# Feature blocks of three matmul operands placed 16, 64 and 8 bytes beyond multiples of 2 KB from each other

## The chip, the cores and the metric

The kernel runs on one core of a Trainium2 chip. The metric is the device time of one execution in microseconds (us), of which three runs are given. The profile is one further execution, seen by the hardware profiler.

## What is computed

Two transformer stacks run one behind the other on 512 tokens of width 1024, in float32. Each has two layers. The reference, cut to what the text speaks of:

```python
def first_block(x, ...):                     # 2 layers
    u = rmsnorm(h, attn_norm[l])
    h = h + hybrid_mixer(u, ...)             # three attention branches, gates, w_o
    u = rmsnorm(h, mlp_norm[l])
    h = h + jnp.square(jax.nn.relu(u @ w_up[l])) @ w_down[l]     # width 4096

def conv_ffn(h, w_up, w_dw, b_dw, w_down):   # second stack, width 2816
    u = depthwise_conv3(h @ w_up) + b_dw
    gate, val = jnp.split(u, 2, axis=-1)
    return (jax.nn.silu(gate) * val) @ w_down
```

The second stack also carries 256 context tokens (through its first layer, and as keys and values in its second).

## The kernel before

**Layout.** Activations lie in SBUF as features: a tile such as `xh` is `[128 partitions, 8 feature blocks (KT), 512 tokens (T)]`, so a feature block is 512 float32 values, 2048 bytes, of each partition, and the eight blocks follow each other without a gap. All weights come as slabs of 2048 values per partition (`wst`, two slots); a slab holds eight blocks of 256 output columns, so two output tiles of 128 columns.

**Arithmetic.** Every large product is made in three passes of the reduced float32 format F32R: an operand is split into a high part and the remainder (`whi`, `wlo` for weights; `xh`, `xl` for the normed input; `uh`, `ul` for the squared halves of the first stack's MLP; `gh`, `gl` for the gated halves of the second stack's; `mh`, `ml` and `oh`, `ol` elsewhere in the first stack; `xch`, `xcl`, `gch`, `gcl` for the 256 context tokens). ScalarE makes the high parts, VectorE (or GpSimd) the remainders. In `products` an output tile of 128 features by 512 tokens takes 24 matmuls: eight times `whi` by head and `whi` by tail (lines 812 and 813), then eight times `wlo` by head (line 816). The stationary operand is a 128x128 piece of a weight slab, the moving operand one feature block. Each matmul has a weight load of its own (LDWEIGHTS, shown as the engine PEld), which overlaps the matmul before it.

```python
for n, k in enumerate(first_ones):
    pe.matmul(out, weights(m.whi, k), head(k), start=opens and n == 0, stop=False)
    pe.matmul(out, weights(m.whi, k), tail(k), start=False, stop=False)
slab_rest()
for k in first_ones:
    last = pe.matmul(out, weights(m.wlo, k), head(k), start=False,
                     stop=closes and k == list(kts)[-1])
```

The same three terms stand in other helpers at lines 822 to 825, 983 to 988, 1060 to 1066 and, on 256 tokens of the second stack, 1290 to 1298. Lines 836 to 838 turn it round: there 128 tokens of `xh` or `xl` are the stationary operand, and `whi` or `wlo` moves.

**Order.** The program of each engine is written out by hand and joined by semaphores; nothing is scheduled by a planner. The DMA queue refills a weight slot when both parts of its slab are made.

**Addresses.** Tiles are placed by hand (`place`), each at the end of the last. `beside_weights(at)` rounds up to an address that is 128 modulo 512, which is also what the addresses of `whi` and `wlo` are; every 128x128 weight piece begins at such an address too, since pieces lie 512 bytes apart. `xh`, `xl`, `uh`, `ul`, `gh`, `gl`, `mh`, `ml`, `oh`, `ol` all begin there, and their blocks follow every 2048 bytes. `xch` and `gch` are placed 64 bytes beyond (`at + 64`), `xcl` and `gcl` right behind them, and their blocks follow every 1024 bytes. `ko` and `Qo` in the attention of the second stack, and `Kw` and `Qw`, are plain F32, and so are the transposes.

Of the kernel before, what the change touches and what calls it, by code (L numbers as in the profile page):

```python
# [23 lines left out]
P = 128  # L24
F32 = mybir.dt.float32
F32R = mybir.dt.float32r
# [6 lines left out]
KT = D // P  # L33
T = 512
# [156 lines left out]
TA = T + TC  # L191
# [222 lines left out]
def place(nc, at, name, shape, dt=F32):  # L414

    return nc.alloc_sbuf_tensor_at(name, shape, dt, offset=at), (at + 4 * int(np.prod(shape[1:])) + 31) // 32 * 32


def beside_weights(at):

    return at + (-at + 16512) % 512
# [7 lines left out]
def two_stacks(nc, io, out):  # L429
    m, s = Names(), Names()  # L430
    with ExitStack() as ctx:

        at = 16512
# [1 line left out]
        m.wst, at = place(nc, at, "wst", [P, 2, SLAB])  # L435
        m.whi, at = place(nc, at, "whi", [P, 2, SLAB], F32R)
        m.wlo, at = place(nc, at, "wlo", [P, 2, SLAB], F32R)
        m.xh, at = place(nc, at, "xh", [P, KT, T], F32R)
        m.xl, at = place(nc, at, "xl", [P, KT, T], F32R)
        m.cst, at = place(nc, at, "cst", [P, 258 + 2 * GATHER])  # L440
        m.sm1, at = place(nc, at, "sm1", [P, 75])
        m.nsink, m.rden, m.nmax = m.sm1[:, 42:58], m.sm1[:, 58:66], m.sm1[:, 66:70]
        m.mods, at = place(nc, at, "mods", [P, DEPTH, 6 * KT * 2])
        region = at = beside_weights(at)
        m.cosT, at = place(nc, region, "cosT", [P, T])
        m.sinT, at = place(nc, at, "sinT", [P, T])
        m.masks, at = place(nc, at, "masks", [P, MASKS])
        a_area = at = beside_weights(at)
        m.AQ, at = place(nc, at, "AQ", [P, 3, T])
        m.AK, at = place(nc, at, "AK", [P, T])  # L450
# [17 lines left out]
        m.mh, _ = place(nc, a_area, "mh", [P, KT, T], F32R)  # L468
        m.ml, _ = place(nc, a_area + 16384, "ml", [P, KT, T], F32R)
        b_area = at = beside_weights(at)  # L470
        assert a_area + 32768 <= b_area
        m.BQK, at = place(nc, at, "BQK", [P, 12, T])
        m.VB, at = place(nc, at, "VB", [P, QB, 12 * HD])
        m.oh, _ = place(nc, b_area, "oh", [P, 9, T], F32R)
        m.ol, _ = place(nc, b_area + 18432, "ol", [P, 9, T], F32R)
        m.uh, _ = place(nc, b_area, "uh", [P, KT, T], F32R)
        m.ul, _ = place(nc, b_area + 16384, "ul", [P, KT, T], F32R)
        work = at
        m.S4, at = place(nc, at, "S4", [P, 4, 4 * P])
        m.PT, at = place(nc, at, "PT", [P, 5, 4 * P])  # L480
        m.rows, at = place(nc, at, "rows", [P, 256])
# [41 lines left out]
        base2 = at = beside_weights(at)  # L523
# [18 lines left out]
        w2_area = at  # L542
# [4 lines left out]
        qs0, at = place(nc, at, "qs0", [P, T])  # L547
        ko1_area = at
        ko1, at = place(nc, at, "ko1", [P, TA])
# [4 lines left out]
        qol1, _ = place(nc, at - 4 * T, "qol1", [P, T], F32R)  # L554
# [17 lines left out]
        qs1, at = place(nc, at, "qs1", [P, T])  # L572
# [3 lines left out]
        ko0, _ = place(nc, ko0_area, "ko0", [P, TA])  # L576
# [2 lines left out]
        m.Kol, at = place(nc, region, "Kol", [P, 2, TA], F32R)  # L579
        qol0, _ = place(nc, at, "qol0", [P, T], F32R)  # L580
        m.Qol = qol0, qol1
        m.gh, at = place(nc, base2, "gh", [P, KT, T], F32R)
        m.gl, at = place(nc, at, "gl", [P, KT, T], F32R)
        m.gch, at = place(nc, at + 64, "gch", [P, KT, TC], F32R)
        m.gcl, at = place(nc, at, "gcl", [P, KT, TC], F32R)
        m.cg, at = place(nc, at, "cg", [P, T])
# [1 line left out]
        m.sgl, at = place(nc, at, "sgl", [P, T])  # L588
        m.gu, at = place(nc, at, "gu", [P, T])
        assert at <= 229344, at  # L590
        n_area = w2_area + 64
        m.sq2, _ = place(nc, n_area, "sq2", [P, 2, T])
        m.sum2, _ = place(nc, w2_area + 12288, "sum2", [P, TA])
        m.xn2, _ = place(nc, n_area + 4096, "xn2", [P, 2, T])
        m.rstd2, _ = place(nc, n_area + 8192, "rstd2", [P, TA])

        psum = ctx.enter_context(nc.psum_tensor("psum", [P, 8 * 512], F32))
        ps = [psum[:, 512 * b:512 * (b + 1)] for b in range(8)]
# [2700 lines left out]
```

## Time and profile before

| what | value |
|---|---|
| runs | 3473.51, 3473.83 and 3475.99 us, median 3473.83 |
| the profiled execution | span 3471.1 us from its first to its last instruction; no other time of it is given |
| TensorE matmul (PE) | busy 3371.9 us, 97% |
| weight loads (PEld) | 2790.2 us, 80% |
| VectorE (DVE) | 2072.0 us, 60% |
| ScalarE (ACT) | 1367.9 us, 39% |
| GpSimd (POOL) | 161.6 us, 5% |
| granted TensorE clock | 0.991 of full speed over the span |

A matmul's own duration in such rows (389 ns for 512 columns) holds its way through the array, which overlaps that of the next one. The time that a matmul costs is the distance from its start to the start of the next, called its pitch below. A row of the timeline that merges several matmuls gives the start of the first; the pitch is then the distance to the start of the row behind it, divided by their count. Engine names in rows: PE, PEld, DVE, ACT, POOL; L812 is line 812.

### The profile page before, as it was taken

How to read it: one execution, taken by the hardware profiler on the slowest of the kernel's cores; microseconds unless marked ns; L12 is line 12 of the kernel's file. 1: busy time of each engine (PE TensorE's matmuls, PEld its weight loads, DVE VectorE, ACT ScalarE, POOL GpSimd, SP SyncE). 2: the span in 40 equal slices, each digit the busy share in tenths (PEclk: the TensorE clock that was granted, in tenths of full speed). 3: DMA queues.
4: the chain of work that ended last, by engine and by line, in shares of the span. 5: the costliest groups of instructions: out<-in, count | busy, mean ns of one | idle time of the engine just before them, and what ended most of it. 6: DMA issues, size and time to landing. Idle time of an engine off the chain costs nothing.

```text
span 3471.1 us, 53538 instructions
## 1 busy us (share of the span) xinstructions
PE 3371.9 (97%) x20066; PEld 2790.2 (80%) x20066; DVE 2072.0 (60%) x3301; ACT 1367.9 (39%) x2166; POOL 161.6 (5%) x39
## 2 busy tenths in 40 slices
PE   8999999999999999999999999999999989999998
PEld 7766888888877678888888777988888878788887
DVE  7876457444678745655576655653544666556546
ACT  6556333222364553322222554342322346534323
POOL 2311000000133010000000000000000000000000
PEclk9999999999999999999999999999999999999999
DMA  4245232222222633332221001121121110122222
GB/s 144 85 158 205 101 121 102 96 96 96 90 103 88 240 124 122 108 119 96 93 92 49 25 14 57 49 73 61 61 73 49 73 61 26 57 69 101 97 97 85
DMA packets 45782, 317.13 MB, mean 91 GB/s; under 512 B 5008, under 2 KB 7312, under 8 KB 8464
## 3 DMA queue, kind: packets, MB, share of 16 engines
q1 hardware_dynamic: 44720, 307.07, 24.8%
q10 hardware_dynamic: 864, 7.31, 0.5%
q8 instruction: 138, 2.26, 0.3%
q14 instruction: 60, 0.49, 0.0%
HBM read 312.26 MB, written 2.10 MB: 91 GB/s over the span
## 4 chain that ended last, share of the span: by engine, by line
PE 84%; DVE 8%; ACT 3%; issue 2%; DVEq 1%; DMA 1%; POOL 0%; SPq 0%; ACTq 0%; POOLq 0%
PE psum L812 22%; PE psum L813 22%; PE psum L816 22%; PE psum L1470 3%; PE psum L1507 2%; PE psum L1491 2%; DVE MA L2478 1%; PE psum L1298 1%; PE psum L896 1%; ACT whi L1692 1%; PE psum L959 1%; PE psum L1290 1%; PE psum L1291 1%; PE psum L936 1%; PE psum L1433 1%
## 5 line engine op out<-in xcount | busy, mean ns | idle before, releaser
L812 PE MATMUL psum<-xh,whi 128*128 128x512 f32 (+1 forms) x2224 | 854.6, 386 | 2.7 <-issue 1.6
L813 PE MATMUL psum<-xl,whi 128*128 128x512 f32 (+1 forms) x2224 | 848.6, 384 | 0.0
L1692 ACT ACTIVATE whi<-wst 128x2048 fp32r<-128x2048 f32 x231 | 441.3, 1910 | 553.0 <-PE psum L816 531.9
L2224 DVE TENSOR_TENSOR wlo<-wst,whi 128x2048 fp32r<-128x2048 f32 x197 | 451.3, 2291 | 173.5 <-ACT whi L1692 171.8
L816 PE MATMUL psum<-xh,wlo 128*128 128x512 f32 (+1 forms) x2224 | 536.4, 383 | 0.1
L812 PEld LDWEIGHTS psum<-xh,whi 128*128 128x128 f32 x2224 | 418.6, 188 | 94.5 <-issue 13.5
L813 PEld LDWEIGHTS psum<-xl,whi 128*128 128x128 f32 x2224 | 418.5, 188 | 81.5 <-issue 1.0
L816 PEld LDWEIGHTS psum<-xh,wlo 128*128 128x128 f32 x2224 | 409.8, 188 | 82.3 <-POOL wlo L777 0.5
L777 POOL TENSOR_TENSOR wlo<-wst,whi 128x2048 fp32r<-128x2048 f32 x34 | 160.9, 4731 | 1081.4 <-ACT whi L1692 1081.1
L812 PE MATMUL psum<-uh,whi 128*128 128x512 f32 x480 | 186.9, 389 | 0.0
L813 PE MATMUL psum<-ul,whi 128*128 128x512 f32 x480 | 186.7, 389 | 0.0
L2083 ACT ACTIVATE S<-S,nmax 128x768 f32<-128x768 f32 (+1 forms) x120 | 101.8, 848 | 112.1 <-DVE rden L2983 85.0
L812 PE MATMUL psum<-gh,whi 128*128 128x512 f32 (+1 forms) x400 | 142.8, 366 | 1.0 <-DVE gl L3161 1.0
L813 PE MATMUL psum<-gl,whi 128*128 128x512 f32 (+1 forms) x400 | 142.2, 364 | 0.0
L1938 ACT ACTIVATE uh<-ur 128x512 f32 x64 | 40.5, 633 | 250.6 <-DVE ur L2726 250.6
L2746 DVE TENSOR_TENSOR hT<-hT,psum 128x512 f32<-128x512 f32 x64 | 43.8, 684 | 136.5 <-PE psum L816 119.5
L3082 DVE SCALAR_TENSOR_TENSOR hT<-psum,mod,hT 128x512 f32<-128x512 f32 (+1 forms) x80 | 51.1, 642 | 123.1 <-PE psum L816 123.0
L812 PE MATMUL psum<-xch,whi 128*128 128x256 f32 x488 | 121.0, 285 | 0.0
L813 PE MATMUL psum<-xcl,whi 128*128 128x256 f32 x488 | 120.3, 283 | 0.0
L816 PE MATMUL psum<-uh,wlo 128*128 128x512 f32 x480 | 119.2, 389 | 0.0
L2975 DVE CUSTOM_DVE_ANT_0 S<-psum,none 128x768 f32<-128x768 f32 (+1 forms) x120 | 101.4, 845 | 27.0 <-PE psum L1470 25.7
L1722 ACT ACTIVATE S<-S,sm 128x257 f32<-128x257 f32 (+5 forms) x144 | 80.4, 558 | 80.8 <-DVE sm L2427 79.2
(415 smaller groups left out, 5898.8 us busy)
## 6 DMA issues: line engine op xcount, KB each, us to landing
wst<-weights SPq DMA_DIRECT2D x287, 1024.0 KB, 4.8
dft<-c_dft ACTq DMA_DIRECT2D x2, 2688.0 KB, 10.1
hT<-x_t SPq DMA_DIRECT2D x4, 512.0 KB, 8.0
wst<-weights SPq DMA_DIRECT2D x2, 512.0 KB, 5.8
cT<-ctx_t ACTq DMA_DIRECT2D x1, 1024.0 KB, 7.0
out<-hT SPq DMA_DIRECT2D x1, 1024.0 KB, 4.9
out<-hT SPq DMA_DIRECT2D x2, 512.0 KB, 3.7
masks<-c_masks SPq DMA_DIRECT2D x1, 644.0 KB, 11.4
```

The lines of the kernel that those rows point to most:

```text
L777: nc.gpsimd.tensor_tensor(m.wlo[:, slab % 2, :], m.wst[:, slab % 2, :], m.whi[:, slab % 2, :].bitcast(F32), ALU.subtract).then_inc(s.lo_re ...
L812: pe.matmul(out, weights(m.whi, k), head(k), start=opens and n == 0, stop=False)
L813: pe.matmul(out, weights(m.whi, k), tail(k), start=False, stop=False)
L816: last = pe.matmul(out, weights(m.wlo, k), head(k), start=False, stop=closes and k == list(kts)[-1])
L1470: last = pe.matmul(ps[2 * par + c // 512][:, 0:w], q[a][:, q0:q0 + P], k[b][:, side * T + c:side * T + c + w], start=(a, b) == terms[0], s ...
L1491: last = pe.transpose(ps[bank][:, b * P:(b + 1) * P], m.S2[:, 2 * (u % 2) + b % 2, kb * P:(kb + 1) * P], ident)
L1507: mm = pe.matmul(ps[6][VH * par:VH * (par + 1), 0:P], m.V4[:, 4 * side + b // 2, col:col + VH], m.PT2[:, CHUNK2[l, u, c] % 5, (b % 4) * P: ...
L1692: act.activation(m.whi[:, slot, :], m.wst[:, slot, :], ACT.Copy).then_inc(s.hi_ready, 1)
L1722: act.activation(sc, sc, ACT.Exp, bias=m.nmax[:, 2 * (u % 2) + par:2 * (u % 2) + par + 1], scale=-1.0, accum_out=m.den[:, 2 * (u % 4) + pa ...
L2083: act.activation(sc, sc, ACT.Exp, bias=m.nmax2[:, 2 * (u % 2) + par:2 * (u % 2) + par + 1], scale=-1.0, accum_out=m.den2[:, c:c + 1]).then ...
L2224: TT(m.wlo[:, slot, :], m.wst[:, slot, :], m.whi[:, slot, :].bitcast(F32), ALU.subtract).then_inc(s.lo_ready, 1)
L2975: nc.vector.tensor_tensor_reduce(m.S2[:, at, 0:w], psum[:, 1024 * par:1024 * par + w], m.none[:, 0:1].broadcast_to([P, w]), -1.0, -TAKEN, ...
```

## The change

Six tiles get rows that are longer than what is used of them: `staggered` allocates `n + step` values for each block and hands out the first `n`. With steps of 4, 16 and 2 values, the blocks of `xh` and `xl` lie 2064 bytes apart, those of `uh` and `ul` 2112, those of `gh` and `gl` 2056. So block k begins 16k, 64k or 8k bytes beyond where it did, relative to its tile. `xl` begins 16512 bytes behind `xh` (128 beyond a multiple of 512 from it); `ul` and `gl` each begin 16896 bytes behind their partner, a multiple of 512. What lies behind the tiles moves: `cst`, `sm1` and `mods` by 256 bytes, `gch` to `gu`, `sq2` and `xn2` by 1024; everything from `region` on stays, for the rounding takes up the difference. `gch` stays 64 bytes beyond an address of the weights' kind. `rstd2`, which nothing reads, is gone. No instruction is added, removed or moved: each engine has as many rows in its program as before (9350 on PE, 2940 on DVE, 1695 on ACT, 10 on POOL, 21 on SP), and only line numbers and operand addresses differ.

```diff
+def staggered(nc, at, name, n, step):
+
+    tile, end = place(nc, at, name, [P, KT, n + step], F32R)
+    return tile[:, :, 0:n], end
...
-        m.xh, at = place(nc, at, "xh", [P, KT, T], F32R)
-        m.xl, at = place(nc, at, "xl", [P, KT, T], F32R)
+        m.xh, at = staggered(nc, at, "xh", T, 4)
+        m.xl, at = staggered(nc, at, "xl", T, 4)
...
-        m.uh, _ = place(nc, b_area, "uh", [P, KT, T], F32R)
-        m.ul, _ = place(nc, b_area + 16384, "ul", [P, KT, T], F32R)
+        m.uh, u_end = staggered(nc, b_area, "uh", T, 16)
+        m.ul, u_end = staggered(nc, u_end, "ul", T, 16)
         work = at
+        assert u_end <= work
...
-        m.gh, at = place(nc, base2, "gh", [P, KT, T], F32R)
-        m.gl, at = place(nc, at, "gl", [P, KT, T], F32R)
+        m.gh, at = staggered(nc, base2, "gh", T, 2)
+        m.gl, at = staggered(nc, beside_weights(at), "gl", T, 2)
+        at = beside_weights(at)
         m.gch, at = place(nc, at + 64, "gch", [P, KT, TC], F32R)
...
-        n_area = w2_area + 64
+        n_area = w2_area + 64 + 1024
         m.sq2, _ = place(nc, n_area, "sq2", [P, 2, T])
         m.sum2, _ = place(nc, w2_area + 12288, "sum2", [P, TA])
         m.xn2, _ = place(nc, n_area + 4096, "xn2", [P, 2, T])
-        m.rstd2, _ = place(nc, n_area + 8192, "rstd2", [P, TA])
```

## Rows read from the trace of the kernel before

**Rows 1.** The page: busy times, slices of the span, and the chain.

```profile
span 3471.1 us, 53538 instructions
PE 3371.9 (97%) x20066; PEld 2790.2 (80%) x20066; DVE 2072.0 (60%) x3301; ACT 1367.9 (39%) x2166; POOL 161.6 (5%) x39
PE   8999999999999999999999999999999989999998
PE 84%; DVE 8%; ACT 3%; issue 2%; DVEq 1%; DMA 1%; POOL 0%; SPq 0%; ACTq 0%; POOLq 0%
```

**Rows 2.** Stretches of 40 us: busy us and (count) by engine, clock, DMA.

```profile
1560.00:1600.00 40.00, 40.00 (x178) 33.14 (x177) 22.28 (x26) 11.77 (x12) 0.00 (x0) 1.00 0.28 100
3240.00:3280.00 40.00, 40.00 (x178) 33.14 (x177) 25.72 (x27) 17.05 (x20) 0.00 (x0) 1.00 0.28 94
```

**Rows 3.** Groups by line and shape: count, busy us, mean ns, idle before.

```profile
L812 PE MATMUL psum<-xh,whi 128*128 128x512 f32 x2096 | 822.9, 393 | 2.7 <-issue 1.6 <-DVE xc L2233 0.8 <-DVE ckvr L2789 0.2
...
L812 PE MATMUL psum<-uh,whi 128*128 128x512 f32 x480 | 186.9, 389 | 0.0
...
L812 PE MATMUL psum<-gh,whi 128*128 128x512 f32 x304 | 118.7, 391 | 1.0 <-DVE gl L3161 1.0
...
L1290 PE MATMUL psum<-xh,whi 128*128 128x256 f32 x256 | 64.8, 292 | 3.6 <-DVE xl L2337 3.6
...
L812 PE MATMUL psum<-xh,whi 128*128 128x256 f32 x128 | 31.7, 285 | 0.0
...
L812 PE MATMUL psum<-gh,whi 128*128 128x256 f32 x96 | 24.0, 286 | 0.0
...
L822 PE MATMUL psum<-uh,whi 128*128 128x512 f32 x32 | 12.4, 389 | 0.0
```

**Rows 4.** Timeline of PE in the first stack: start, us, instruction.

```profile
1499.62 0.39 PE L813 MATMUL psum<-xl,whi 128*128 128x512 f32 x1
1499.85 0.39 PE L812 MATMUL psum<-xh,whi 128*128 128x512 f32 x1
...
1502.57 1.98 PE L816 MATMUL psum<-xh,wlo 128*128 128x512 f32 x8
1504.38 0.39 PE L812 MATMUL psum<-xh,whi 128*128 128x512 f32 x1
```

**Rows 5.** Timeline of PE: 256 tokens of `xh`, blocks beside the weights.

```profile
2183.45 1.12 PE L816 MATMUL psum<-xh,wlo 128*128 128x256 f32 x8
2184.41 0.28 PE L812 MATMUL psum<-xh,whi 128*128 128x256 f32 x1
```

**Rows 6.** Timeline of PE: 256 tokens of `gch`, 64 bytes beyond.

```profile
2370.07 0.28 PE L812 MATMUL psum<-gch,whi 128*128 128x256 f32 x1
...
2371.72 0.98 PE L816 MATMUL psum<-gch,wlo 128*128 128x256 f32 x7
2372.54 0.40 PE L812 MATMUL psum<-gh,whi 128*128 128x512 f32 x1
```

**Rows 7.** Timeline of PE: `xch`, then the first matmuls of a `xh` tile.

```profile
2293.36 1.10 PE L816 MATMUL psum<-xch,wlo 128*128 128x256 f32 x8
2294.30 0.40 PE L812 MATMUL psum<-xh,whi 128*128 128x512 f32 x1
2294.54 0.39 PE L813 MATMUL psum<-xl,whi 128*128 128x512 f32 x1
2294.76 0.39 PE L812 MATMUL psum<-xh,whi 128*128 128x512 f32 x1
2294.99 0.40 PE L813 MATMUL psum<-xl,whi 128*128 128x512 f32 x1
2295.23 0.39 PE L812 MATMUL psum<-xh,whi 128*128 128x512 f32 x1
2295.46 0.40 PE L813 MATMUL psum<-xl,whi 128*128 128x512 f32 x1
2295.69 0.39 PE L812 MATMUL psum<-xh,whi 128*128 128x512 f32 x1
2295.92 0.39 PE L813 MATMUL psum<-xl,whi 128*128 128x512 f32 x1
2296.15 0.39 PE L812 MATMUL psum<-xh,whi 128*128 128x512 f32 x1
```

**Rows 8.** Timeline of PE: plain F32 logits (`ko`, `Qo`: 512, 256, 512, 256 columns).

```profile
1912.12 1.46 PE L1470 MATMUL psum<-ko,Qo 128*128 128x512 f32 x4
1913.41 0.60 PE L1491 MATMUL psum<-cst,S 128*128 128x128 f32 x4
```

**Rows 9.** Who waited for the matmuls of line 816 (us, times).

```profile
  ACT whi L1692: 531.9, 74
  ACT cv L2193: 150.8, 49
  DVE hT L3082: 123.0, 54
  DVE hT L2746: 119.5, 32
```

## The prediction

> **What bounds the kernel now.** I read the page first. TensorE is busy for 97% of the span, every slice but a few is full, and the chain that ended last is 84% PE [rows 1]. Next the stretches: within an MLP, PE is busy for all 40.00 of 40.00 us at a granted clock of 1.00 of full speed (the 2.4 GHz level), while DVE works 22 to 26 us and ACT 12 to 17, with the DMA engines at 0.28 [rows 2]. Then who waits for whom: ScalarE's next weight half and the residual additions of VectorE wait for PE's last matmul of a tile (531.9, 123.0 and 119.5 us in total) [rows 9], and not the other way round. So the end is set by how many matmuls there are and by the distance from the start of one to the start of the next. The change touches nothing but that distance.
>
> **The pitch before.** In the timeline of a long run of tiles the start moves from 1499.62 to 1504.38 us over 21 matmuls of 512 columns (13 single ones and the 8 merged), so 226.7 ns each [rows 4]. 512 columns at one column per cycle of 2.4 GHz are 213.3 ns. Each matmul therefore loses 13.3 ns, 5.9%, which no semaphore explains. Three things in the rows say what sort of loss that is:
>
> - It does not grow with the columns. `xh` with 256 columns: 2183.45 to 2184.41 us for 8 matmuls, 120.0 ns [rows 5], which is 13.3 ns above 106.7.
> - It changes with the address of the moving operand. `gch` has the same shape, the same weights and the same program around it, but lies 64 bytes beyond the weights' residue: 2370.07 to 2372.54 us for 21 matmuls, 117.6 ns [rows 6]. `xch`, with the same 64 bytes: 2293.36 to 2294.30 us for 8, 117.5 ns [rows 7]. That is 2.4 ns less per matmul. (Those blocks are also 1 KB long and not 2 KB apart; the rows don't separate the two.)
> - It hangs on the reading rate. Plain F32 takes two cycles a column: 1536 columns in four matmuls are 1.280 us, and they take 1912.12 to 1913.41, 1.29 us, so about 2.5 ns lost by each [rows 8].
>
> My reading: while a matmul streams a block at full rate, the weight load of the next one reads SBUF too, and some of its reads hold up the stream. How many do depends on how the two addresses run against each other. Before the change that relation is the same for every one of these matmuls, since pieces and blocks are all 128 modulo 512; after it every block k has its own.
>
> **A rule against this.** The Trainium skill says in "TensorE: Matmul & The Clock Gate", Part 2, that the moving operand and the weight load have independent read ports, so that loading weights takes nothing from the running matmul, and gives N/2.4 + 2.5 ns as the distance, 215.8 ns for 512 columns. By that rule addresses would not count and the time would stay at 3473.8 us. This trace disagrees with its figure for F32R (226.7 ns) and agrees with it for plain F32 (about 2.5 ns).
>
> **How much each ns is worth.** Matmuls of 512 columns that take one of the six tiles as moving operand: 2096 in each of the three terms for `xh` and `xl`, 480 in each for `uh` and `ul`, 304 in each for `gh` and `gl`, and 32 more in each for `uh` (the tile that is multiplied at line 822) [rows 3]. The rest of `xh` (lines 822 to 825, 983 to 988, 1060 to 1066) are 144, by the program. That is 6288 + 1440 + 912 + 96 + 144 = 8880 matmuls, 8.9 us for every ns of pitch; 6432 of them are `xh` and `xl`, 1536 `uh` and `ul`, 912 `gh` and `gl`. Of 256 columns there are (256 + 128 + 96) x 3 = 1440 [rows 3], 1.4 us per ns. Together they are 8880 x 226.7 + 1440 x 120.0 = 2186 us of the span.
>
> **The change part by part.**
>
> - The staggered starts of moving operands: the price has no row of its own. The nearest rows are the 64-byte tiles at 256 columns, 2.4 ns below the aligned ones [rows 5 to 7]. Since the loss does not grow with columns, I carry that over: 8880 x 2.4 = 21.3 us, and 1440 x 2.4 = 3.5 us. Sum: 24.8 us less.
> - Lower bound of the cost: the loss falls to the 2.5 ns of the plain F32 matmuls [rows 8]. 10.8 ns x (8880 + 1440) = 111 us less.
> - Upper bound: the row of unsettled pitches. After a switch from `xch` the first `xh` matmul takes 240 ns, and the six from 2294.54 to 2295.92 take 230 ns each, in an uneven order; only then it settles at 226.7 [rows 7]. If with eight different relations it never settles, 3.3 ns x 8880 = 29 us more.
> - `xh` and `xl` as stationary operand (lines 836 to 838, 192 matmuls), `cst` moved by 256 bytes, `gch` and the rest by 1024 with their residue kept: nothing. The first are too few (1 ns each is 0.2 us), the others keep the residue or are plain F32, which loses little anyway [rows 8].
> - VectorE's and ScalarE's writes of the six tiles at new starts: nothing. PE hides them; in the stretches DVE is idle for 14 to 18 of 40 us and ACT for 23 to 28 [rows 2]. They would have to grow by more than half before anybody waits.
> - A faster PE asks for slabs sooner. A slab lasts 48 matmuls, 10.9 us; its refill and its halves are covered by DMA at 0.28 and the idle shares above [rows 2]. So a gain on PE is passed on whole where PE is full, and I take it whole.
>
> The sum goes against the profiled span: 3471.1 - 24.8 = 3446.3 us. The median of the runs, 3473.83, is 2.7 us above that span; I add it: 3449 us, and round to 3450.
>
> **Rivals.**
>
> 1. *A small gain, as priced* (3450 us, faster). For: two tiles each side of a difference of 2.4 ns. Against: it is a constant offset there, and at 256 columns a weight load covers nearly the whole matmul, at 512 only the first half.
> 2. *A large gain* (3363 to 3435, say 3410). The aligned start may be the worst of all relations, each block and each part hitting it anew. If half of 13.3 ns goes, 6.7 x 8880 + 6.7 x 1440 = 69 us less, 3405. For: 2.5 ns shows that the loss can nearly vanish. Against: the 64 bytes took away only 2.4 of 13.3.
> 3. *Slower: the stream no longer settles.* Place: every 512-column tile of `xh`, two thirds of PE's matmuls of that kind. Price: pitch 230 instead of 226.7, 3474 + 29 = 3503 us; with 8 bytes (half of what a 16-byte step gives) for `gh` alone it would be only 3 us. For: right after a switch the pitch swings between 220 and 240 ns (the rows round to 10) and every mean over it lies above the settled one [rows 7]. Against: the 256-column tiles with another relation are faster, not slower. It decides when the mean pitch of staggered tiles is above 226.7.
> 4. *No change*: the loss belongs to the format, and the 2.4 ns at 256 columns come from the 1 KB blocks, not from the 64 bytes. Then nothing in the six tiles, whose blocks stay 2 KB long, gets cheaper: 3474 us. This is also where the skill's rule on separate ports would lead.
>
> **How the numbers follow.** A measurement of this kernel tells 0.2%, 7 us, from no change; that is 0.7 ns of pitch. Chances: case 1 0.40, case 2 0.22, case 3 0.23, case 4 0.15. Cases 1 and 2 are faster, 0.62; case 4 same, 0.14 with a little of it slower; slower 0.24. The range leaves out the lower part of case 2 (below 3390, more than 8 ns of pitch) and the upper part of case 3: from 3390 to 3490 us. Case 1 by itself would be 3435 to 3462.
>
> **What would show it.** In the profile after, the merged row of eight `xh` matmuls of line 816, from its start to the start of the next row and divided by eight: 224.3 ns if I am right, 226.7 if case 4 holds, 230 with visible swings for case 3, below 222 for case 2. `mh`, `ml`, `oh` and `ol` are not touched and must stay at 226.7. `gh` (8 bytes), `xh` (16) and `uh` (64) give three steps side by side: if the relation of addresses matters, they should differ. Busy PE should fall by what the span falls by, and DVE and ACT durations should stay. I am wrong if the pitch of all three tiles stays the same, or if the gain shows elsewhere than in these matmuls.

## The result, and the profile after

The changed kernel takes 3502.84 us (3500.40 to 3502.89, three runs) against 3473.83. The ratio is 1.0079, with a 95% interval of 1.0061 to 1.0097: 0.8% slower, 29 us, where 24 us less was forecast. That is the time of the rivals' case 3, which had been worked out at 3503 us; what is left of its reason is said below.

The page of the changed kernel, against [rows 1]. Its lines are numbered seven higher from the matmul helpers on (L812 is now L819, L813 L820, L816 L823).

```profile
span 3501.1 us, 53538 instructions
PE 3402.8 (97%) x20066; PEld 2784.8 (80%) x20066; DVE 2072.5 (59%) x3301; ACT 1367.0 (39%) x2166; POOL 160.6 (5%) x39
...
PE 85%; DVE 8%; ACT 3%; issue 2%; DVEq 1%; DMA 1%; SPq 0%; ACTq 0%
```

The span grew by 30.0 us and PE's busy time by 30.9; VectorE and ScalarE stay where they were. The loss lies in matmuls alone. The groups by line and shape (count, busy us, mean ns), against [rows 3]:

```profile
L819 PE MATMUL psum<-xh,whi 128*128 128x512 f32 x2096 | 831.7, 397 | 2.5 <-issue 1.6 <-DVE xc L2240 0.6 <-DVE ckvr L2796 0.2
L820 PE MATMUL psum<-xl,whi 128*128 128x512 f32 x2096 | 826.0, 394 | 0.0
L823 PE MATMUL psum<-xh,wlo 128*128 128x512 f32 x2096 | 525.9, 392 | 0.0
L819 PE MATMUL psum<-uh,whi 128*128 128x512 f32 x480 | 189.0, 394 | 0.0
...
L819 PE MATMUL psum<-gh,whi 128*128 128x512 f32 x304 | 119.9, 394 | 0.8 <-DVE gl L3168 0.8
L819 PE MATMUL psum<-xch,whi 128*128 128x256 f32 x488 | 118.1, 283 | 0.0
...
L819 PE MATMUL psum<-mh,whi 128*128 128x512 f32 x128 | 49.8, 389 | 0.0
```

Over its three terms `xh`/`xl` with 512 columns grew by 25.0 us, `uh`/`ul` by 5.8, `gh`/`gl` by 4.5. The untouched `mh` has its 389 ns and 49.8 us as before. Matmuls of 256 columns got cheaper, the 1440 on staggered tiles by 3.3 us together. `xch` and `xcl` won 6.6 us, although neither their addresses nor their program changed; `gch` and `gcl` lost 1.9.

These busy times hold each matmul's way through the array, so they don't add up to the span. Summed from start to start over all matmuls of the two traces, the account closes: `xh` and `xl` with 512 columns take 23.0 us more, `uh` and `ul` 6.3, `gh` and `gl` 4.5, all matmuls of 256 columns on the tiles named 4.5 less, everything else 0.5 more, together 29.8. By its settled pitch `xh` would have lost 30 us (4.7 ns on 6432 matmuls); 7 us of that don't show, 5 of them because fewer of its matmuls waited or ran at the 1.2 GHz level in this execution: 24 stood 400 to 440 ns from the next one before, 5 after.

The timeline of a long run, against [rows 4], shows the pitch: from 1509.93 to 1513.64 us 16 matmuls, then 8 in 1.84 us.

```profile
1509.93 0.39 PE L819 MATMUL psum<-xh,whi 128*128 128x512 f32 x1
1510.16 0.39 PE L820 MATMUL psum<-xl,whi 128*128 128x512 f32 x1
1510.39 0.40 PE L819 MATMUL psum<-xh,whi 128*128 128x512 f32 x1
...
1513.64 2.00 PE L823 MATMUL psum<-xh,wlo 128*128 128x512 f32 x8
1515.48 0.39 PE L819 MATMUL psum<-xh,whi 128*128 128x512 f32 x1
```

24 matmuls in 5.55 us are 231.3 ns each, where 226.7 stood. The median over all tiles of 24 is 231.4 ns for `xh`, 230.9 for `uh` and 232.5 for `gh`. Inside a tile the single distances swing between 225 and 237 ns; before they were 226 or 227.

### The profile page after: what moved, and what is told of

The parts are those of the page before. It is cut to its first block, busy times and chain, and to the rows that moved or that the text cites. A ratio compares the mean times of both kernels' runs of the same rounds, so it can differ in the third digit from the quotient of the medians.

```text
span 3501.1 us, 53538 instructions
## 1 busy us (share of the span) xinstructions
PE 3402.8 (97%) x20066; PEld 2784.8 (80%) x20066; DVE 2072.5 (59%) x3301; ACT 1367.0 (39%) x2166; POOL 160.6 (5%) x39
## 4 chain that ended last, share of the span: by engine, by line
PE 85%; DVE 8%; ACT 3%; issue 2%; DVEq 1%; DMA 1%; SPq 0%; ACTq 0%
PE psum L819 22%; PE psum L820 22%; PE psum L823 22%; PE psum L1477 2%; PE psum L1514 2%; PE psum L1498 2%; DVE MA L2485 1%; PE psum L903 1%; PE psum L1305 1%; PE psum L966 1%; ACT whi L1699 1%; PE psum L1297 1%; PE psum L1298 1%; DVE BQK L2249 1%; PE psum L943 1%
## 5 line engine op out<-in xcount | busy, mean ns | idle before, releaser
L819 PE MATMUL psum<-xh,whi 128*128 128x512 f32 (+1 forms) x2224 | 863.0, 390 | 2.5 <-issue 1.6
L820 PE MATMUL psum<-xl,whi 128*128 128x512 f32 (+1 forms) x2224 | 857.0, 388 | 0.0
L823 PE MATMUL psum<-xh,wlo 128*128 128x512 f32 (+1 forms) x2224 | 543.7, 386 | 0.0
L819 PEld LDWEIGHTS psum<-xh,whi 128*128 128x128 f32 x2224 | 417.5, 188 | 104.7 <-issue 13.3
L820 PEld LDWEIGHTS psum<-xl,whi 128*128 128x128 f32 x2224 | 418.4, 188 | 89.2 <-issue 1.0
L823 PEld LDWEIGHTS psum<-xh,wlo 128*128 128x128 f32 x2224 | 409.7, 188 | 89.3 <-POOL wlo L784 0.2
L819 PE MATMUL psum<-uh,whi 128*128 128x512 f32 x480 | 189.0, 394 | 0.0
L820 PE MATMUL psum<-ul,whi 128*128 128x512 f32 x480 | 188.4, 393 | 0.0
L819 PE MATMUL psum<-gh,whi 128*128 128x512 f32 (+1 forms) x400 | 143.7, 368 | 0.8 <-DVE gl L3168 0.8
L820 PE MATMUL psum<-gl,whi 128*128 128x512 f32 (+1 forms) x400 | 144.0, 369 | 0.0
L823 PE MATMUL psum<-uh,wlo 128*128 128x512 f32 x480 | 121.2, 393 | 0.0
L819 PE MATMUL psum<-xch,whi 128*128 128x256 f32 x488 | 118.1, 283 | 0.0
L820 PE MATMUL psum<-xcl,whi 128*128 128x256 f32 x488 | 117.3, 281 | 0.0
```

## The experiments

**How a pitch was measured by itself.** Five small programs hold nothing but TensorE's part: weights and blocks filled once, then tiles of 24 matmuls in the kernel's own pattern. They compute nothing of the reference. Each row of a table has its own source line, so each case is a group in the trace. In the first four programs it runs four tiles behind one tile of the plain layout; the fifth, in section 6, puts a tile of 512 columns before each tile of 256. The core of it:

```python
def case(n=512, at=0, step=0, gap=None, block=2048, w=0):
    pitch = block + step                      # bytes between blocks
    return n, at, pitch, KT * pitch if gap is None else gap, w
CASES = [
    ("plain", case(), lambda pe, *a, **o: pe.matmul(*a, **o)),
    ("osixteen", case(at=16), lambda pe, *a, **o: pe.matmul(*a, **o)),
...
    ("both", case(at=64, w=64), lambda pe, *a, **o: pe.matmul(*a, **o)),
```

**1. The first table.**

> A kernel of its own: TensorE alone, the kernel's 24-matmul pattern (hi by head and tail, then lo by head), four tiles per row of a table, each behind one tile of the plain layout. Each row of the table has its own source line. It computes nothing of the reference. Theory U (a relation of addresses that changes from matmul to matmul keeps the pitch from settling): with 512 columns the plain layout 226.7 ns; all blocks 8 to 1024 bytes off but 2048 apart also 226 to 227.5, since the relation is constant; steps of 8, 16, 32, 64, 128, 256 bytes 229 to 233; steps of 512 and 1024 bytes 226.7. Theory R (each relation of moving and weight address has its own price, and the aligned one is a cheap one): constant offsets of 16 to 256 bytes cost 229 to 233 as well, and moving the weights by the same 64 bytes as the blocks brings 226.7 back. Theory B (blocks that are not 2 KB apart cost, whatever the weights): steps of 512 and 1024 bytes cost 229 to 233 too. With 256 columns: 117.5 with 64 bytes of offset and 120.0 without, for blocks 2 KB and 1 KB apart alike, if the address makes that difference; else the 1 KB blocks alone show 117.5.

The timeline of this program; of each case the starts of its second and third tile, 24 matmuls apart. L25 is an offset of 16 bytes, L26 of 32, L29 of 256, L32 the tail alone 64 bytes on, L36 blocks with a step of 16, L41 with a step of 512, L43 weights alone 64 on, L44 weights and blocks both 64 on, L45 and L46 256 columns at offsets 0 and 64.

```profile
98.26 3.87 PE L25 MATMUL psum<-data,whi 128*128 128x512 f32 x16
...
103.82 3.87 PE L25 MATMUL psum<-data,whi 128*128 128x512 f32 x16
...
126.02 3.90 PE L26 MATMUL psum<-data,whi 128*128 128x512 f32 x16
...
131.62 3.90 PE L26 MATMUL psum<-data,whi 128*128 128x512 f32 x16
...
209.06 3.79 PE L29 MATMUL psum<-data,whi 128*128 128x512 f32 x16
...
214.50 3.79 PE L29 MATMUL psum<-data,whi 128*128 128x512 f32 x16
...
291.20 3.87 PE L32 MATMUL psum<-data,whi 128*128 128x512 f32 x16
...
296.76 3.87 PE L32 MATMUL psum<-data,whi 128*128 128x512 f32 x16
...
401.21 3.87 PE L36 MATMUL psum<-data,whi 128*128 128x512 f32 x16
...
406.76 3.87 PE L36 MATMUL psum<-data,whi 128*128 128x512 f32 x16
...
538.92 3.79 PE L41 MATMUL psum<-data,whi 128*128 128x512 f32 x16
...
544.37 3.79 PE L41 MATMUL psum<-data,whi 128*128 128x512 f32 x16
...
593.48 3.90 PE L43 MATMUL psum<-data,whi 128*128 128x512 f32 x16
...
599.08 3.90 PE L43 MATMUL psum<-data,whi 128*128 128x512 f32 x16
...
621.23 3.79 PE L44 MATMUL psum<-data,whi 128*128 128x512 f32 x16
...
626.67 3.79 PE L44 MATMUL psum<-data,whi 128*128 128x512 f32 x16
...
645.88 2.08 PE L45 MATMUL psum<-data,whi 128*128 128x256 f32 x16
...
648.76 2.08 PE L45 MATMUL psum<-data,whi 128*128 128x256 f32 x16
...
662.82 2.05 PE L46 MATMUL psum<-data,whi 128*128 128x256 f32 x16
...
665.64 2.05 PE L46 MATMUL psum<-data,whi 128*128 128x256 f32 x16
```

A constant offset is not free: 5.56 us over 24 is 231.7 ns at 16 bytes, 5.60 is 233.3 at 32. At 256 it is 226.7 again, and so are steps of 256, 512 and 1024 bytes. Weights moved alone give 233.3 (5.60 us), weights and blocks moved together 226.7. Theory U had constant offsets at 226 to 227.5 ns and theory B had costly steps of 512 and 1024 bytes; neither is so. R stands, but for its 229 to 233 ns at 256 bytes: the price repeats after 256 bytes.

A change of relation from one matmul to the next is not free either. With the tail alone 64 bytes on, 16 of 24 matmuls stand at offset 0 and 8 at 64, which by the prices of constant offsets would be 227.4 ns in the mean; 5.56 us over 24 are 231.7. With the tail 16 bytes on, 228.3 would be the mean and 231.1 was measured; at 128 bytes the mean of prices, 228.9, is met.

With 256 columns 64 bytes save 2.3 ns (120.0 to 117.6), for blocks 1 KB or 2 KB apart alike: the prediction's reading of rows 5 and 6 was right. At 512 columns the same 64 bytes cost 2.2 ns.

**2. Undoing the largest part; a constant offset in the kernel.** `x_plain` puts the two `staggered` calls of `xh` and `xl` back to `place`. `all_64`:

```diff
-        m.xh, at = place(nc, at, "xh", [P, KT, T], F32R)
+        m.xh, at = place(nc, at + 64, "xh", [P, KT, T], F32R)
...
-        m.gch, at = place(nc, at + 64, "gch", [P, KT, TC], F32R)
+        m.gch, at = place(nc, at, "gch", [P, KT, TC], F32R)
```

and the same 64 bytes for `uh`, `ul` and `gh`.

> The changed kernel with xh and xl put back to blocks 2048 bytes apart; uh, ul, gh and gl stay staggered. By the pitches of the changed kernel's trace xh and xl hold some 29 us of the loss on 6432 matmuls of 512 columns, against a few us that 256-column matmuls win, so 3476 to 3482 us. Rival (the loss comes from uh, ul, gh, gl or from the tiles that moved): 3495 us or more.

> The kernel before with xh, xl, uh, ul, gh and gl each begun 64 bytes further on and blocks still 2048 bytes apart, so that the moving operand is always 64 bytes off the weights' residue. Theory U: the relation is constant, so the 512-column pitch stays 226 to 227.5 ns and the time within 7 us of before, at most 3 us less by the 256-column matmuls. Theory R (any relation but the aligned one costs): pitch 229 to 233 and 3495 to 3520 us. The prediction's own price (64 bytes save 2.4 ns of every matmul): 224.3 ns and 3450 us.

`x_plain`: 3486.86 us, ratio to before 1.0037 (1.0023 to 1.0051). So the loss is there in part without the `xh` stagger, and `xh` holds 18 us of the span (3501.1 to 3482.9), not the 21 to 27 forecast: by busy time its 512-column matmuls gave back 25 us, but `xch` and `xcl` lost the 6.5 that they had won. `all_64`: 3487.77 us, 1.0035 (1.0024 to 1.0045), pitch 228.8 by its timeline (8 matmuls from 1664.09 to 1665.92 us, 1.83 us over 8), near the 228.9 that the first table has for 64 bytes. U had said at most 3482, R at least 3495, so neither range of times is met. R's took a dearer offset than the table gives; by the table it is 2.2 ns on 8880 matmuls less 2.3 on 1440, 16 us, and 13 were measured between the medians (3474.58 to 3487.77). The prediction's own 224.3 ns and 3450 us are refuted.

**3. The scan, and a stagger that keeps the residue.**

> TensorE alone as in the first table, none of the reference computed. With 512 columns: 24 to 248 bytes and 320 of constant offset between blocks and weights; with 256 columns ten offsets; with 128, 384 and 448 columns offsets 0, 64 and 192; weight pieces of 64 and 32 columns in place of 128; and 32 plain F32 matmuls each at offsets 0, 64 and 128. Theory R (the price hangs on moving address minus weight address modulo 256): 320 bytes cost what 64 cost, 228.9 ns, 192 bytes what the weights moved by 64 cost, 233.3; no offset is below 226.7 with 512 columns. Theory L (each line of the weight load that meets the stream costs about one cycle of 2.4 GHz, so the loss scales with weight columns): pieces of 64 columns 219 to 221 ns, of 32 columns 215 to 218. If the loss belongs to the format, it stays 13.3 ns there. Plain F32: 429 ns at every offset. With 384 and 448 columns the aligned loss is 13.3 ns too; with 128 the weight load is as long as the matmul and the pitch is its own.

```diff
-        m.uh, _ = place(nc, b_area, "uh", [P, KT, T], F32R)
-        m.ul, _ = place(nc, b_area + 16384, "ul", [P, KT, T], F32R)
+        uh, u_end = place(nc, b_area, "uh", [P, KT, T + 64], F32R)
+        ul, u_end = place(nc, u_end, "ul", [P, KT, T + 64], F32R)
+        m.uh, m.ul = uh[:, :, 0:T], ul[:, :, 0:T]
```

> The kernel before with uh and ul alone staggered, their blocks 2304 bytes apart (256 bytes beyond 2 KB in place of the change's 64), which keeps every block at the weights' address modulo 256. Theory R: pitch 226.7 on uh and ul and the time within 2 us of before (3472 to 3477). Theory U (any block by block change of relation unsettles the pitch): 230 to 231 ns on 1536 matmuls, 5 to 7 us more, 3479 to 3482 us.

`u_256`: 3473.99 us, 0.9998 (0.9989 to 1.0007), and `uh` at the pitch of before. Its group, against 121.2 us with 64 bytes of step and 119.2 before:

```profile
L817 PE MATMUL psum<-uh,wlo 128*128 128x512 f32 x480 | 119.2, 389 | 0.0
```

A block-by-block change of 256 bytes costs nothing. The prices of this scan and of the first and third tables, settled pitch in ns at 512 columns, by blocks' minus weights' address:

| bytes | 0 | 4 | 8 | 12 | 16 | 24 | 32 | 40 | 48 | 64 | 80 | 96 |
|---|---|---|---|---|---|---|---|---|---|---|---|---|
| ns | 226.7 | 236.7 | 233.3 | 229.2 | 231.7 | 233.0 | 233.3 | 232.5 | 233.3 | 228.9 | 231.1 | 233.3 |

| bytes | 112 | 128 | 144 | 160 | 176 | 192 | 208 | 224 | 240 | 256 | 320 | 1024 |
|---|---|---|---|---|---|---|---|---|---|---|---|---|
| ns | 231.1 | 233.3 | 233.3 | 234.3 | 231.1 | 233.3 | 234.7 | 233.3 | 233.3 | 226.7 | 228.9 | 226.7 |

Of 31 offsets tried below 256 bytes (those not shown lie between 230.8 and 234.8) none is cheaper than the aligned one. At 256 columns it is among the dearest: 120.0 at 0, 96 and 128, 118.7 at 16, 116.7 at 32, 118.3 at 48, 117.8 at 64 and 192, 117.1 at 240. At 448 columns 64 bytes give 200.0 against 202.7; at 384 both give 173.3, and 192 bytes 176.7. So the sign of an offset's price depends on the columns. The loss of the aligned layout against one column per cycle of 2.4 GHz is not 13.3 ns throughout either, as had been forecast: it is at 384 columns, but 16.0 at 448.

Theory L falls. Fewer weight columns make it slower: with weights of 64 columns (L58, first and fourth tile) 72 matmuls in 16.56 us are 230.0 ns; with 32 columns (L59) two tiles stand 5.55 us apart, 231.3, and the mean over its tiles is 231.7.

```profile
841.04 3.84 PE L58 MATMUL psum<-data,whi 128*64 128x512 f32 x16
...
857.60 3.84 PE L58 MATMUL psum<-data,whi 128*64 128x512 f32 x16
...
874.12 3.87 PE L59 MATMUL psum<-data,whi 128*32 128x512 f32 x16
...
879.67 3.87 PE L59 MATMUL psum<-data,whi 128*32 128x512 f32 x16
```

Plain F32 is the same at offsets 0, 64 and 128: 429.1 ns from record to record. (32 matmuls show as 64 records; each record is half of a plain F32 matmul. Rows 8 are four such halves, two of 512 columns and then two of 256, so the 2.5 ns lost by each record stand, but a matmul has two of them.)

**4. Is it the difference alone, and can context tiles gain?**

> TensorE alone as in the first tables, none of the reference computed. (1) Blocks and weights both 128 or both 192 bytes on, and weights 256 on with blocks 64: theory R (the price hangs on the difference alone) 226.7, 226.7 and 233.3 (difference -192 is 64: 228.9); blocks 128 with weights 64 as a difference of 64, 228.9; weights 192 on with plain blocks as -192, so 64, 228.9. (2) Further constant offsets between 4 and 232 bytes: none below 226.7. (3) One block used by all matmuls, or one for head and one for tail: 226.7 at offset 0 and the same prices at 16 to 128 as with eight blocks (231.7, 233.3, 228.9, 233.3), if the relation to the weights alone counts; other prices if it is the relation of one block to the next. (4) The same weight piece for all eight: 226.7. (5) Weight pieces read with a stride of two values, so that their address runs as fast as the moving one: no forecast from R; if the loss comes from the two addresses passing each other, the pitch falls at some offset below 226.7. (6) 256 columns with blocks 1 KB apart: 116.7 at 32 bytes, 117.7 at 64.

All of theory R's forecasts are met: 226.7 with both 128 or both 192 on; 228.9 with blocks 128 and weights 64 on, with weights 192 on, and with weights 256 and blocks 64 on; and two blocks, one for all heads and one for all tails, show 226.7, 231.7, 233.3, 228.9 and 233.3 at 0, 16, 32, 64 and 128 bytes. So where the offset is constant, the distance from one block to the next plays no part. Weights read with a stride of two: 231.5 to 233.3, no offset helps.

> The kernel before with xch, xcl, gch and gcl 32 bytes beyond the weights' residue in place of 64, blocks 1 KB apart as before. By the scan 32 bytes give 116.7 ns at 256 columns against 117.7 at 64, on 664 x 3 = 1992 matmuls: 2 us less, 3472 us, less than a run can tell. Rival (the pitch there is set by how a tile starts, not by the offset): no row of 116.7 and 3474 us.

`ctx_32` (each of the four context tiles 32 bytes earlier): 3474.19 us, 1.0000 (0.9991 to 1.0009). The row of 116.7 is there in most `xch` tiles (67.2 us for 488 `wlo` matmuls against 67.6), and as forecast a run cannot tell it.

**5. Which weight load, and does the table carry over?**

> TensorE alone as in the first tables, none of the reference computed. Which weight load meets a stream: that of the next matmul (theory N, the reading of the prediction) or the matmul's own (theory O)? In the rows own64, own128 and own16 every second matmul has block and weights both 64, 128 or 16 bytes on; in next64, next128 and next16 the block of a matmul matches the weights of the one behind it. N: next64, next128 and next16 226.7 ns, and own64, own128 and own16 above it. O: the reverse. weights and blocks rows move one side of every second matmul alone; both theories 228 to 231. steps: blocks and weight pieces both staggered by 16 bytes; O 226.7, N about 231, since the piece behind is always 16 bytes further. 96 columns of weights at offset 0 between 226.7 and 230.0, by the two rows measured for 128 and 64. 480 to 504 columns: 213 to 224 ns, a loss of 13 to 16 ns like that at 448 and 384.

Neither theory: with 64 bytes own and next both 231.7, with 128 bytes 228.3 and 230.0, with 16 bytes 233.3 and 230.5; moving only the weights of every second matmul by 16 bytes costs nothing (226.7), by 128 bytes it gives 233.3. Staggering blocks and weights alike gives 229.4. In the own rows and in this last one every block agrees with its own weights, and yet they cost 1.7 to 6.7 ns: the difference of a matmul's two addresses sets the price alone only where it and the addresses' residue stay the same from matmul to matmul. Of the other forecasts, weights of 96 columns came out at 230.0, the upper end; 480 and 496 columns at 216.7 and 220.0; 504 columns at 226.7, above the 224 allowed. The reading "the next weight load disturbs the stream" is neither shown nor refuted by these pairs; a simple rule of own or next load is. The rows own64 (L24) and next64 (L25), second and third tile:

```profile
71.75 3.87 PE L24 MATMUL psum<-data,whi 128*128 128x512 f32 x16
...
77.31 3.87 PE L24 MATMUL psum<-data,whi 128*128 128x512 f32 x16
...
99.44 3.87 PE L25 MATMUL psum<-data,whi 128*128 128x512 f32 x16
...
105.00 3.87 PE L25 MATMUL psum<-data,whi 128*128 128x512 f32 x16
```

> The kernel before with xh, xl, uh, ul, gh and gl each begun 32 bytes further on, blocks 2048 bytes apart. If the table of prices carries over to the kernel: 233.3 ns on 8880 matmuls of 512 columns, 59 us more; 116.7 instead of 120.0 ns on 1440 of 256 columns, 5 us less; so about 3528 us, 3518 to 3533. If constant relations are cheap in the kernel, under 3490.

`all_32` (as `all_64`, with 32; `gch` keeps its 64): 3518.26 us, 1.0123 (1.0105 to 1.0141), at the lower end of the forecast. Its settled pitch is the table's: the median over tiles of 24 is 233.3 ns for `xh`, `uh` and `gh` alike (228.9 in `all_64`). The groups of its `wlo` matmuls show the price on the moved tiles, and none on `mh`:

```profile
L816 PE MATMUL psum<-xh,wlo 128*128 128x512 f32 x2096 | 531.9, 395 | 0.0
L816 PE MATMUL psum<-uh,wlo 128*128 128x512 f32 x480 | 122.3, 395 | 0.0
...
L816 PE MATMUL psum<-mh,wlo 128*128 128x512 f32 x128 | 32.2, 389 | 0.0
```

**6. Untouched context tiles that got faster.** Eleven times in the kernel 96 matmuls of `xch` and `xcl` follow each other, ten times of them behind a tile of 512 columns. These ten go at 113.3 ns in the changed kernel, where all eleven go at 117.8 before; in `x_plain` they are back at 117.8.

> TensorE alone, none of the reference computed. Tiles of 256 columns, 64 bytes off the weights, each behind a tile of 512 columns, as the context tiles stand in the second stack. In the changed kernel untouched context tiles run at 113 ns where before they run at 118, so a constant relation seems to have more than one settled pitch, and the tile in front to choose. If so, a row whose tile in front lies 16, 32 or 128 bytes off, or is staggered by 16, shows 113 where the aligned one in front shows 118; and perhaps another offset of block 0, block 7 or the tail tips it over with an aligned tile in front, which a kernel could use: 4.4 ns on up to 1992 matmuls, 9 us. Rival: the 118 stands in every row with an aligned tile in front, and only the offsets within the tile change it, by what the scan gave (116.7 to 120).

In the small program the forecast holds in part: behind an aligned tile of 512 columns the 64-byte tile settles at 117.9 ns; behind one at 64 bytes, or staggered by 16, at 113.3; behind one at 16 or 128 bytes at 117.9. Behind one at 32 bytes (L23; the start of the 256-column tile and of the next 512-column tile) the first of four still ran at 117.9 and the other three at 113.3:

```profile
72.42 2.05 PE L23 MATMUL psum<-data,whi 128*128 128x256 f32 x16
...
75.25 3.88 PE L115 MATMUL psum<-data,whi 128*128 128x512 f32 x16
...
80.84 1.98 PE L23 MATMUL psum<-data,whi 128*128 128x256 f32 x16
...
83.56 3.89 PE L115 MATMUL psum<-data,whi 128*128 128x512 f32 x16
```

2.83 us and 2.72 us for the same 24 matmuls: one relation of addresses, two settled pitches. The kernels bear out a part of it: in `all_32` the same ten go at 113.3 as well, but in `all_64`, where `xh` is 64 bytes off, they stay at 117.8. Of one of them the starts of the first and second tile (24 matmuls in 2.82 us, 117.5 ns each):

```profile
2292.34 0.28 PE L812 MATMUL psum<-xch,whi 128*128 128x256 f32 x1
...
2295.16 0.28 PE L812 MATMUL psum<-xch,whi 128*128 128x256 f32 x1
```

So the offset of the tile in front is not all that chooses; what else does was not found. With an aligned tile in front, block 0 alone at the weights' residue gave 115.0 over the tile. That was tried in the kernel:

```diff
-        m.xch, at = place(nc, at + 64, "xch", [P, KT, TC], F32R)
+        xch, at = place(nc, at, "xch", [P, 16 + KT * TC], F32R)
+        m.xch = Blocks(xch, [0] + [16 + k * TC for k in range(1, KT)], TC)
```

> The kernel before with block 0 of xch alone put at the weights' own residue, the other seven and all of xcl left 64 bytes off; all else as before. In the table of entries this took a 256-column tile behind an aligned 512-column tile from 117.9 to 115.0 ns a matmul. xch has 488 x 3 = 1464 matmuls: 4.2 us less, 3470 us, about half of what a run can tell, so the pitch in the trace has to show it: 113 to 115 ns in the tiles of xch in place of 117.5. Rival: in the kernel the tile in front ends otherwise than in the small program, the pitch stays at 117.5 to 118 and the time at 3474.

`ctx_first`: 3475.63 us, 1.0002 (0.9993 to 1.0011), no difference that a run can tell. In the trace the starts of the first three of four tiles of `xch` that follow each other:

```profile
2289.42 0.28 PE L824 MATMUL psum<-xch,whi 128*128 128x256 f32 x1
...
2292.18 0.28 PE L824 MATMUL psum<-xch,whi 128*128 128x256 f32 x1
...
2295.00 0.28 PE L824 MATMUL psum<-xch,whi 128*128 128x256 f32 x1
```

The first tile takes 2.76 us, 115.0 ns each, as in the small program; the second 2.82 us, and by the starts 117.4 and the two behind it 117.5. So the effect of block 0 did carry over, but only to a tile right behind one of 512 columns: 13 tiles have it, 312 of 1464 matmuls, worth 0.9 us (2.9 ns each). The forecast had counted all 1464. The group of `xch` at `wlo` cannot show it: it is 69.2 us, with a mean of 284 ns, against 67.6 and 279 before, but just so in `u_256`, where nothing of `xch` was moved. The difference lies in `xch` tiles behind a wait, at the 1.2 GHz level (219 ns a matmul in `ctx_first` from 1830.5 us on, at a granted clock of 0.50); these two executions have more of them. No kernel here beats the one before.

## Why the prediction was wrong

- **What bounds the kernel, and what a ns is worth: right.** PE's busy time and the span moved together, 30.9 and 30.0 us. But 8880 x 1 ns is not all of it: counted from start to start, 512-column matmuls of the six tiles took 33.8 us more and the 256-column ones gave 4.5 back.
- **That the pitch hangs on the address of the moving block: right,** and on its difference to the weights' address, modulo 256 and not 512. The reading behind it, that the next matmul's weight load holds up the stream, is not shown: its forecast for the pairs (226.7 for next64, next128 and next16) was missed in all three (231.7, 230.0 and 230.5).
- **"Since the loss does not grow with columns, I carry that over": this step failed.** The 2.4 ns that 64 bytes save at 256 columns are real (2.3 measured), but at 512 columns they are 2.2 ns of cost. Equal losses of 13.3 ns at two lengths did not mean equal prices of an offset. The 21.3 us that this term of the sum took off should have been some 42 us on top (4.7, 4.2 and 5.8 ns on `xh`, `uh` and `gh`, of which 33.8 us show in the account).
- **The size.** By the table of prices `xh` takes offsets 0 to 112 in steps of 16 (mean 231.2 ns) and `xl` 128 to 240 (233.3); weighted 16 to 8 that is 231.9, and 231.4 was measured. `uh` and `ul` take 0, 64, 128 and 192, which makes 230.6 against 230.9. `gh` and `gl`, with 8 bytes of step, take 0 to 56, about 232, against 232.5. So the means of prices of constant offsets come within 0.5 ns here. That is not a rule: with the tail alone 64 or 16 bytes on they fall short by 4.3 and 2.8 ns.
- **Case 3 had the right number,** 3503 us, in part by luck. Its 230 ns was taken from the few matmuls after a switch of tiles. The kernels with constant offsets (228.9 and 233.3 ns) show a loss of this kind without any change from block to block, and the swings that case 3 named as its sign are no proof of it: at a constant 16 bytes the distances swing too, between 227 and 235 ns in a cycle of four. How much of the 4.2 to 5.8 ns comes from the changes themselves is not shown. And the range, 3390 to 3490 us, left out case 3's own price, though it had been given 0.23.
- **Rival 2 rested on a wrong thought,** that the aligned start may be the worst. At 512 columns it is the best of all tried; the 2.5 ns of plain F32 are reached by none of the offsets tried.
- **The edits costed at nothing stand:** VectorE and ScalarE keep their durations. `cst` moved by 256 bytes, a multiple of the period.
- **The rule on separate ports** (the Trainium skill, "TensorE: Matmul & The Clock Gate", Part 2) says that a weight load takes no read bandwidth from the running matmul. At 512 columns of F32R the pitch changes when the weights alone are moved (233.3 ns with 64 bytes, 226.7 without), so the two reads are not independent here. For plain F32 the pitch is the same at the three offsets tried.

What stays open is the mechanism: why 256 bytes, why the sign turns with the columns, why fewer weight columns are slower, what a change of relation costs, and what picks one of two settled pitches.

## What to carry to other kernels

A price per instruction taken from a row of another shape can have the wrong sign. Where a layout question turns on a few ns of a regular stream, a program with a table of cases, one source line each, answers some forty of them in about a millisecond on the chip (1057.79 us for the scan); build it before the kernel is edited. For F32R matmuls of 512 columns, keep all moving blocks and all weight pieces at one and the same address modulo 256 bytes: that was the cheapest of all layouts tried, while pairs that agree only each with its own weights cost 228.3 to 233.3 ns. And a mean over a group mixes tiles at two clocks; whether a small effect carried over is read from the starts of single tiles.

## What the runs showed of the hardware

- F32R matmuls back to back: 226.7 ns at 512 columns when the addresses of all blocks and weights agree modulo 256 bytes, up to 236.7 (a constant 4 bytes) when not; plain F32 shows no such dependence (429.1 ns per record at 0, 64 and 128 bytes).
- An agreement that holds only for each matmul by itself is not enough: 231.7, 228.3 and 233.3 ns when every second matmul has both addresses 64, 128 or 16 bytes on.
- 256 columns: 120.0 ns aligned, 116.7 at 32 bytes. 448 columns: 202.7 aligned, 200.0 at 64 bytes.
- Many settled pitches are multiples of 3.33 ns: 226.7 (68), 230.0 (69), 233.3 (70), 120.0 (36), 116.7 (35), 113.3 (34), 216.7 at 480 columns (65), 220.0 at 496 (66). 512 and 504 columns both take 226.7 ns.
- The same 256-column tile, 64 bytes off, settles at 117.9 or 113.3 ns. In the small program the tile in front decides it in most rows; in `all_64` it stays at 117.8 behind tiles for which the small program shows 113.3.
